# Four edits to a two-block transformer kernel: where the modulation product is made, in which order the score passes of differential attention run, where embedding and mixing are done, and how retention steps through its heads

## The chip, the cores and the metric

The kernel runs on one core of one Trainium2 chip, as one program of some twenty phases. The metric is the device time of one execution in microseconds (us), given as the median of three runs.

## The reference, cut to what matters

The sequence has 1,024 tokens of 1,024 float32 values. The first block is a mixing layer (differential and neighbourhood attention), a routed mixture of experts, and a gated embedding; the second block is two layers of retention and stick-breaking attention whose norm is modulated by a product of a condition vector.

```python
def diff_attention(...):          # 4 heads, two score maps of width 64 each
    s1 = einsum(q[..., 0, :], k1) * scale ; s2 = einsum(q[..., 1, :], k2) * scale
    w = softmax(s1) - lam * softmax(s2) ; o = w @ v
    return rms_norm(o, g_sub) * (1.0 - lam_init)

def first_block(...):
    h = h + concatenate([oa, ob]) @ w_out
    h = h + hier_moe(rms_norm(h, g_ffn), w_rg, w_re, w1, w3, w2)   # 2 of 32 experts a token
    h = h + rms_norm(p @ w_ple, g_ple) * sigmoid(rms_norm(h, g_plg) @ w_plg)

def hybrid_layer(x, c_act, ...):  # twice; c_act = silu(c)
    shift, scale, gate = split(c_act @ w_ada + b_ada, 3)           # w_ada: 1024 x 3072
    h = rms_norm_2(x, norm_g) * (1.0 + scale) + shift
    proj = h @ w_in
    y = concatenate([retention(...) * silu(rg), stick_breaking(...) * silu(sg)]) @ w_out
    return x + gate * y
# retention: 4 heads of 128, per head  o -> (o - mean(o)) * rsqrt(var(o) + eps)
```

## The kernel before, in words

All work is float32. A product that needs the accuracy is made as three passes over operands split into a high and a low part (`_hi`, `_lo`). Tokens go in 8 tiles of 128 (`NT`). Each phase opens its own buffers, gives each of the five engines one stream of instructions, written out by hand with semaphores between them, and ends with all engines waiting for each other. So nothing of a phase starts before the last instruction and the last waited-for transfer of the phase ahead. Names in the trace carry the tag of their phase: `da_` differential attention, `na_` neighbourhood attention, `rt_` router, `ex_` experts, `bt_` between, `ple_gate_`, `in_`, `ret_`, `stick_`, `out_`, `fin_`.

**Differential attention.** `score(i, t)` (L1204) makes the two score maps of one tile, c = 0 and c = 1, each of two 512-column halves `n` and three passes, into two pairs of PSUM banks. Map c waits for `exped[c]`, the exponential that reads the bank of the tile before. VectorE takes two maxima (L1310), ScalarE two exponentials (L1247), VectorE combines (L1324), TensorE turns the weights (L1229) and multiplies by v (L1237). `score(i+1, t+1)` stands in front of the turn and product of tile t. GpSimd lays the bias of the next phase (L1402) meanwhile.

**Router.** Per tile, TensorE turns the normed x (L687) and multiplies with 36 logit columns (L707). Behind the logits stand the modulation products (`modulate`, L695: 16 pieces of `w_ada`, 1,536 KB each, with 8 buffers, loaded by SyncE at L572), with the rank products (L718) after nine of them. VectorE ranks the experts; GpSimd then scatters 16 lots of slot rows (L628). **Experts** stream 192 MB of weights. **Between**, one tile after another, mixes the two expert rows of each token into h (L1801, L1806), makes `p @ w_ple` (L1764), its norm and gain (`factor`, L1822), and stores both; they are read again by the next phase.

**Gate phase** (`dense_phase` with tag `ple_gate`). For column block 0, tile t is loaded by GpSimd, squared on ScalarE (L221), its root taken (L224), scaled on VectorE in place (L315), turned on TensorE (L450), cast to the high part (L228), and subtracted for the low part (L326); then 24 matmuls a column block (L461 to L463). VectorE's order in the loop is take(t+1), scale(t+2), then the output of t. Column block 1 uses the kept operands.

**Retention.** Per head, in a loop: ScalarE copies the turned q and k, TensorE makes decayed scores, chunk products and outputs (L1898, L1905, L1914, L1917), and VectorE does the decay of q (L1961), the masked scores (L1966), the states (L1973, L1977), and the norm of the output in whole-head steps of 128x1024 (L1989 to L1997) and the gate (L2000). One set of buffers serves all heads.

## Time and profile before

| | |
|---|---|
| median of three runs | 3539.03 us (3537.36 to 3544.37) |
| profiled execution | 3547.53 us, span 3545.9 us |
| busy: TensorE / VectorE / ScalarE / GpSimd | 84% / 44% / 34% / 8% |
| differential attention | 310 to 593 us |
| router | 966 to 1078 us |
| experts | 1078 to 1684 us |
| between | 1684 to 1756 us |
| gate | 1756 to about 1889 us |
| retention, first and second layer | 2267 to 2350 and 3086 to 3169 us |

TensorE is busiest over the whole, but each phase has its own bound, and the phases do not overlap. So a change is to be read phase by phase, from the first instruction of one to the first of the next. Times of rows are from the start of the span. The profiled execution is 8.5 us longer than the median of the runs.

### The profile page before, as it was taken

Reading aid. Unit: us, or ns where it says so; the run is one execution under the profiler, and the core shown is the slowest. Engines: PE = TensorE matmul, PEld = TensorE weight load, DVE = VectorE, ACT = ScalarE, POOL = GpSimd, SP = SyncE. Lnnn points to the kernel's source line nnn. Section 1 sums busy time; section 2 is a strip of 40 time slices with the busy share of each in tenths; the row PEclk is TensorE's granted clock in tenths of the full one; section 3 lists DMA queues with packets and bytes.
Section 4 is the critical chain, followed back from the end, with each engine's and each line's share of the span. In section 5 each row is a group of like instructions: output and inputs, shape, how many; then the busy total and the mean of one; then the engine's idle time right before and its main releaser. Section 6 shows DMA issues by size and latency. Waiting matters only on the chain. (4 is left out here: it accounts for less than half of the span.)

```text
span 3545.9 us, 61528 instructions
## 1 busy us (share of the span) xinstructions
PE 2976.0 (84%) x22494; PEld 2317.5 (65%) x22494; DVE 1569.1 (44%) x2788; ACT 1199.3 (34%) x2129; POOL 276.9 (8%) x453
## 2 busy tenths in 40 slices
PE   7997876877876999998497999868877999868876
PEld 6786664655755888886275888644466888754455
DVE  4852656776131222221445411268844421068853
ACT  4332544665120110000253222148832222128841
POOL 0002600000022111111100000000000000000000
PEclk9998987988968999999798999879988999979998
DMA  5113112111397999998944222341044222241034
GB/s 178 68 71 105 27 25 94 35 56 54 118 372 281 394 395 394 395 394 309 348 156 163 93 96 72 117 133 33 10 158 158 103 95 74 99 145 35 25 116 163
DMA packets 244095, 545.93 MB, mean 154 GB/s; under 512 B 29196, under 2 KB 110896, under 8 KB 217240
## 3 DMA queue, kind: packets, MB, share of 16 engines
q1 hardware_dynamic: 213960, 460.23, 35.9%
q0 software_dynamic: 26720, 75.77, 6.5%
q10 hardware_dynamic: 3312, 8.59, 0.6%
q8 instruction: 60, 0.98, 0.1%
q14 instruction: 43, 0.35, 0.0%
HBM read 437.66 MB, written 107.79 MB: 154 GB/s over the span
## 5 line engine op out<-in xcount | busy, mean ns | idle before, releaser
L461 PE MATMUL ps<-in_wh,in_xh 128*128 (+1 forms) x1024 | 400.8, 391 | 0.0
L462 PE MATMUL ps<-in_wl,in_xh 128*128 (+1 forms) x1024 | 399.1, 390 | 0.0
L463 PE MATMUL ps<-in_wh,in_xl 128*128 (+1 forms) x1024 | 399.0, 390 | 0.0
L463 PEld LDWEIGHTS ps<-in_wh,in_xl 128*128 128x128 f32 x1024 | 192.7, 188 | 40.2
L462 PEld LDWEIGHTS ps<-in_wl,in_xh 128*128 128x128 f32 x1024 | 192.9, 188 | 39.8
L461 PEld LDWEIGHTS ps<-in_wh,in_xh 128*128 128x128 f32 x1024 | 192.8, 188 | 39.6
L1026 DVE TENSOR_TENSOR ex_hid<-ps,ex_act 32x128 f32<-32x128 f32 x96 | 28.2, 294 | 328.7 <-PE ps L1073 327.9
L461 PE MATMUL ps<-mix_in_wh,mix_in_xh 128*128 (+1 forms) x384 | 152.2, 396 | 9.1 <-DVE mix_in_out L381 5.6
L463 PE MATMUL ps<-mix_in_wh,mix_in_xl 128*128 (+1 forms) x384 | 150.1, 391 | 0.0
L462 PE MATMUL ps<-mix_in_wl,mix_in_xh 128*128 (+1 forms) x384 | 150.1, 391 | 0.0
L245 ACT COPY in_out<-ps 128x512 f32<-128x512 f32 x64 | 37.6, 588 | 248.3 <-PE ps L463 248.3
L304 DVE TENSOR_TENSOR in_wl<-in_raw,in_wh (+1 forms) x64 | 44.2, 690 | 159.9 <-ACT in_wh L216 159.7
L2325 DVE TENSOR_TENSOR stick_w<-stick_z,ps 128x256 f32<-128x256 f32 (+2 forms) x96 | 91.7, 955 | 52.2 <-PE ps L2159 50.6
L304 DVE TENSOR_TENSOR in_wl<-early,in_wh x64 | 43.1, 689 | 160.7 <-ACT in_wh L216 160.7
L1035 DVE COPY ex_y<-ps 32x256 f32<-32x256 f32 x96 | 41.0, 427 | 162.1 <-PE ps L1100 161.2
L206 POOL DMA_DIRECT2D out_x<-y x4 | 2.1, 528 | 1314.5 <-POOLq L36 1314.5
L461 PE MATMUL ps<-out_wh,out_xh 128*128 128x512 f32 x256 | 101.8, 398 | 0.9 <-DVE out_xl L326 0.9
L463 PE MATMUL ps<-out_wh,out_xl 128*128 128x512 f32 x256 | 100.5, 392 | 0.0
L462 PE MATMUL ps<-out_wl,out_xh 128*128 128x512 f32 x256 | 100.3, 392 | 0.0
L2318 DVE TENSOR_TENSOR stick_lo<-stick_soft,stick_hi 128x256 fp32r<-128x256 f32 (+2 forms) x96 | 91.6, 955 | 15.1 <-ACT stick_hi L2248 13.8
L988 ACT COPY ex_xT<-ps 128x768 f32<-128x768 f32 x33 | 26.4, 799 | 212.1 <-PE ps L1052 212.1
L2253 ACT ACTIVATE stick_w<-stick_w 128x256 f32<-128x256 f32 (+2 forms) x96 | 81.3, 847 | 46.0 <-DVE stick_w L2325 42.2
(409 smaller groups left out, 7433.7 us busy)
## 6 DMA issues: line engine op xcount, KB each, us to landing
ex_w_w1a<-in_w_dram SPq DMA_DIRECT2D x32, 1024.0 KB, 13.3
ex_w_w1b<-in_w_dram SPq DMA_DIRECT2D x32, 1024.0 KB, 14.4
ex_w_w3a<-in_w_dram SPq DMA_DIRECT2D x32, 1024.0 KB
ex_w_w3b<-in_w_dram SPq DMA_DIRECT2D x32, 1024.0 KB
ex_w_w2a<-in_w_dram SPq DMA_DIRECT2D x32, 1024.0 KB, 14.4
ex_w_w2b<-in_w_dram SPq DMA_DIRECT2D x32, 1024.0 KB
proj<-in_out SPq DMA_DIRECT2D x128, 256.0 KB, 2.0
rt_w_ada<-in_w_ada_dram SPq DMA_DIRECT2D x16, 1536.0 KB, 22.0
```

The lines of the kernel that those rows point to most:

```text
L206: pool.dma_start(x[p][:, 0:NK * P], src[p * P:(p + 1) * P, 0:NK * P]).then_inc(x_loaded[p], 16)
L245: act.copy(out[p][:], k.ps[:, 2 + p, :]).then_inc(out_ready, 1)
L304: dve.tensor_tensor(wl[:, c % 2, bass.ds(kt, 1), :], raw[c % 2][:, bass.ds(kt, 1), :], wh[:, c % 2, bass.ds(kt, 1), :].bitcast(F), ALU.sub ...
L461: pe.matmul(o, xh[:, kt, tok], wb[0], start=(kt == 0), stop=False)
L462: pe.matmul(o, xh[:, kt, tok], wb[1], start=False, stop=False)
L463: last = pe.matmul(o, xl[:, kt, tok], wb[0], start=False, stop=(kt == KT - 1))
L988: act.copy(xT[:].rearrange("p b k n -> p b (k n)"), psX).then_inc(x_taken, 1)
L1026: dve.tensor_tensor(hid[group(g), HM:], psH[1][BR:P, g * HQ:(g + 1) * HQ], act1[BR:P, g * HQ:(g + 1) * HQ], ALU.mult)
L1035: dve.tensor_copy(y[group(g), YM:], psY[BR:P, g * YQ:(g + 1) * YQ])
L2253: act.activation(ap, ap, ACT.Exp).then_inc(w_done, 1)
L2318: dve.tensor_tensor(lo[n % 2][:, :, cols(n)], soft[n % 2][:, :, cols(n)], hi[n % 2][:, :, cols(n)].bitcast(F), ALU.subtract).then_inc(lo_d ...
L2325: dve.tensor_tensor(w[n % 2][:, :, cols(n)], z[n % 3][:, :, cols(n)], psT[:, :, cols(n)], ALU.subtract).then_inc(weighed, 1)
```

## The change

Four edits, all of them moves or regroupings; what is computed stays.

1. The modulation product moves from the router to differential attention. It is cut into 32 pieces of 768 KB, one for each tile of each head, with 4 buffers. `modulate(h, t)` is 4 matmuls of 384 columns. Bias and gain are put on by GpSimd, which also stores the result.
2. The twelve score matmuls of a tile alternate between the two maps, whose operands lie on the lower and the upper 64 partitions, and all wait for both exponentials.
3. The phase between is gone. The embedding (`p @ w_ple`, norm, gain) goes into the router, its products behind the logits and behind the ranks. The mixing goes into the gate phase, on VectorE ahead of the square; the mixed x is stored by GpSimd, and the expert rows have one buffer each.
4. Retention keeps two sets of buffers and runs heads in pairs; the row statistics are taken by `bn_stats` and `bn_aggr`, and the normalised output is made by ScalarE.

```diff
@@ differential attention, TensorE
             def score(i, t):
-                for c in range(2):
-                    half = slice(c * DQK, (c + 1) * DQK)
-                    if not isinstance(i, int) or i > 0:
-                        pe.wait_ge(exped[c], i)
-                    for n in range(2):
-                        for i_pass, (q, kk) in enumerate(((q_hi, k_hi), (q_lo, k_hi), (q_hi, k_lo))):
+                if not isinstance(i, int) or i > 0:
+                    pe.wait_ge(exped[0], i)
+                    pe.wait_ge(exped[1], i)
+                for n in range(2):
+                    for i_pass, (q, kk) in enumerate(((q_hi, k_hi), (q_lo, k_hi), (q_hi, k_lo))):
+                        for c in range(2):
+                            half = slice(c * DQK, (c + 1) * DQK)
...
+            def modulate(h, kt):
+
+                pe.wait_ge(ada_loaded[kt % WB], 16 * (KT // WB * h + kt // WB + 1))
+                if kt == 0:
+                    pe.wait_ge(row_taken, h)
+                for g in range(GROUPS):
+                    last = pe.matmul(psM[g * GP:(g + 1) * GP, :], c_act[:, kt, :], wb[kt % WB][:, g * QN:(g + 1) * QN],
+                                     start=(kt == 0), stop=(kt == KT - 1))
+                last.then_inc(ada_used, 1)
...
                 for t in range(NT):
                     i = NT * h + t
+                    modulate(h, t)
                     if t + 1 < NT:
                         score(i + 1, t + 1)
@@ router, TensorE
+                if t % 2 == 1:
+                    pe.wait_ge(pr_loaded, 16)
+                    turn_p(t // 2)
...
-            for i in range(KT):
-                modulate(i)
-            pe.wait_ge(row_taken, 2)
-            modulate(KT)
+            pe.wait_ge(p_taken, NT // 2)
+            pe.wait_ge(w_p_loaded, 32)
+            embed(0)
+            embed(1)
...
-            for i in range(KT + 1, LAYERS * KT):
-                modulate(i)
+            for t in range(2, NT):
+                embed(t)
@@ router, VectorE
+            weigh(0)
             dve.wait_ge(ranked, 1)
...
+            for t in range(1, NT):
+                weigh(t)
@@ gate phase, GpSimd
+            if mixed:
+                for t in range(NT):
+                    p, own = t % 2, slice(t * P, (t + 1) * P)
+                    if t >= 2:
+
+                        pool.wait_ge(x_ready, t - 1)
+                        pool.wait_ge(x_saved[p], 16 * (t // 2))
+                    pool.dma_start(x[p][:], src[own, :]).then_inc(x_loaded[p], 16)
+                    if t >= 1:
+                        pool.wait_ge(x_mixed, t)
+                    for i in range(TOP_K):
+                        pool.dma_start(ye[i][:], k.slot_y[i * SEQ + t * P:i * SEQ + (t + 1) * P, :]).then_inc(ye_loaded, 16)
+                    if t >= 1:
+                        pool.dma_start(resid[(t - 1) * P:t * P, :], x[1 - p][:]).then_inc(x_saved[1 - p], 16)
@@ gate phase, ScalarE
             def scale(t, p, j):
                 if norm:
-                    act.wait_ge(x_loaded[p], 16 * (j + 1))
+                    if mixed:
+                        act.wait_ge(x_mixed, t + 1)
+                    else:
+                        act.wait_ge(x_loaded[p], 16 * (j + 1))
@@ gate phase, VectorE
                             take(2 * j + p + 1, 1 - p)
+                            mix(2 * j + p + 2, p, j + 1)
                             scale(2 * j + p + 2, p)
@@ retention, TensorE
+            turn(0)
+            score(0)
+            turn(1)
+            score(1)
+            for h in range(HR):
+                output(h)
+                if h + 2 < HR:
+                    turn(h + 2)
+                if h == 1:
+                    score(2)
+                    score(3)
@@ retention, VectorE
-                link(dve.tensor_reduce(sums[:], o, X, ALU.add))
-                link(dve.tensor_scalar(mu[:], sums[:], 1.0 / DR, None, ALU.mult))
-                link(dve.tensor_tensor(cen[:], o, each(mu[:]), ALU.subtract))
-                link(dve.tensor_tensor(sq[:], cen[:], cen[:], ALU.mult))
-                link(dve.tensor_reduce(var_sum[:], sq[:], X, ALU.add))
...
+                for t in range(a, b):
+                    last = dve.bn_stats(stats[p][:, t, :], psX[p][:, tile(t)])
+                last.then_inc(stats_done, 1)
+                dve.wait_ge(stats_done, u + 1)
+                for t in range(a, b):
+                    last = dve.bn_aggr(moments[p][:, t, :], stats[p][:, t, :])
...
@@ retention, ScalarE
+                for t in range(a, b):
+                    last = act.activation(nrm[p][:, tile(t)], psX[p][:, tile(t)], ACT.Identity, scale=rs[p][:, t:t + 1],
+                                          bias=shift[p][:, t:t + 1])
```

On TensorE in differential attention, at the first two tiles of a head, the program of before has all six score matmuls of one map and then all six of the other (`da_k_hi`, `da_q_lo` and so on are the high and low parts of k and q):

```order
L1204 MATMUL ps<-da_k_hi,da_q_hi 128x512
L1204 MATMUL ps<-da_k_hi,da_q_lo 128x512
L1204 MATMUL ps<-da_k_lo,da_q_hi 128x512
L1204 MATMUL ps<-da_k_hi,da_q_hi 128x512
L1204 MATMUL ps<-da_k_hi,da_q_lo 128x512
L1204 MATMUL ps<-da_k_lo,da_q_hi 128x512
```

The changed program has there:

```order
L1314 MATMUL ps<-da_k_hi,da_q_lo 128x512 x2
L1314 MATMUL ps<-da_k_lo,da_q_hi 128x512 x2
L1298 ISA
L1302 MATMUL ps<-da_w_ada,da_c_act 32x384 x4
L1308 REGISTER_ALU
L1314 MATMUL ps<-da_k_hi,da_q_hi 128x512 x2
L1314 MATMUL ps<-da_k_hi,da_q_lo 128x512 x2
```

Each pass now comes as a pair, one matmul for each map, and the four modulation matmuls stand between the scores of one tile and the next.

On VectorE in the gate phase, from the take of tile t+1 to the output of tile t, the program of before has:

```order
L326 ISA
L326 TENSOR_TENSOR ple_gate_xl<-ps,ple_gate_xh 128x8x128
L310 REGISTER_ALU
L311 ISA
L311 TENSOR_SCALAR ple_gate_ms<-ple_gate_ss 128x1
L313 ISA
L313 RECIPROCAL ple_gate_rs<-ple_gate_sd 128x1
L315 SCALAR_TENSOR_TENSOR ple_gate_x<-ple_gate_x,ple_gate_rs,ple_gate_gain 128x1024
```

The changed program has, from the second mixing step to the next take and mixing (`ple_gate_ye` are the expert rows, `ple_gate_xs` the scaled copy):

```order
L346 SCALAR_TENSOR_TENSOR ple_gate_x<-ple_gate_ye,slot_w,ple_gate_x 128x1024
L353 ISA
L353 TENSOR_SCALAR ple_gate_ms<-ple_gate_ss 128x1
L355 ISA
L355 RECIPROCAL ple_gate_rs<-ple_gate_sd 128x1
L360 SCALAR_TENSOR_TENSOR ple_gate_xs<-ple_gate_x,ple_gate_rs,ple_gate_gain 128x1024
...
L371 ISA
L371 TENSOR_TENSOR ple_gate_xl<-ps,ple_gate_xh 128x8x128
L342 ISA
L343 ISA
L343 SCALAR_TENSOR_TENSOR ple_gate_x<-ple_gate_ye,slot_w,ple_gate_x 128x1024
```

Two steps of 128x1024 stand now between the take and the mean square, which waits for ScalarE's square of what they make.

On VectorE in retention, at the end of a head, the program of before has:

```order
L1990 TENSOR_SCALAR ret_mu<-ret_sums 128x8
L1991 TENSOR_TENSOR ret_cen<-ps,ret_mu 128x1024
L1992 TENSOR_TENSOR ret_sq<-ret_cen 128x1024
L1993 TENSOR_REDUCE ret_var_sum<-ret_sq 128x8
L1994 TENSOR_SCALAR ret_ms<-ret_var_sum 128x8
L1996 RECIPROCAL ret_rs<-ret_sd 128x8
L1997 TENSOR_TENSOR ret_nrm<-ret_cen,ret_rs 128x1024
```

The changed program has, around the end of the first pair:

```order
L2005 SCALAR_TENSOR_TENSOR ret_shift<-ret_moments,ret_rs 128x8
L2013 TENSOR_TENSOR ret_y<-ret_nrm,ret_g 128x8x128
L1970 TENSOR_TENSOR ret_qTd<-ret_qT,ret_q_dec 128x1024
L1974 TENSOR_TENSOR ret_sm<-ps,ret_dec 128x512 x2
L1979 COPY ret_state<-ps 128x128
L1983 SCALAR_TENSOR_TENSOR ret_state<-ret_state,ret_t_dec,ps 128x128 x6
L2013 TENSOR_TENSOR ret_y<-ret_nrm,ret_g 128x8x128
```

The large centring, squaring and normalising steps are gone from VectorE, and the gate of one head stands beside the start of a later one.

## Rows read from the trace of the kernel before

**Rows 1.** By stretch: us, busy of PE, PEld, DVE, ACT, POOL, clock, DMA share, GB/s.

```profile
966.00:1078.00 112.00, 69.77 (x454) 49.43 (x454) 34.45 (x84) 23.60 (x40) 32.78 (x39) 0.63 0.82 318
1756.00:1889.00 133.00, 101.13 (x448) 82.70 (x448) 55.54 (x83) 60.12 (x85) 5.25 (x10) 0.87 0.50 168
2267.00:2350.00 83.00, 47.24 (x304) 44.09 (x304) 50.42 (x76) 15.13 (x26) 0.00 (x0) 0.75 0.43 133
```

**Rows 2.** Timeline of the phase between and its end: start, us, instruction [idle before].

```profile
1683.77 1.28 ACT L1777 ACT_TABLE_LOAD   x1 [17.00 <-PEq L36]
1695.87 1.28 DVE L1801 SCALAR_TENSOR_TENSOR bt_mid<-bt_expert,slot_w,bt_h 128x1024 f32<-128x1024 f32 x1 [18.98 <-DMA bt_expert<-slot_y]
1697.18 1.28 DVE L1806 SCALAR_TENSOR_TENSOR bt_out<-bt_expert,slot_w,bt_mid 128x1024 f32<-128x1024 f32 x1
1751.70 0.34 ACTq L1790 DMA_DIRECT2D ple<-bt_factor  x1
1756.33 1.28 ACT L262 ACT_TABLE_LOAD   x1 [6.18 <-PEq L36]
```

**Rows 3.** Tile view of the expert rows of the phase between.

```profile
DMA to landing us min/median/max: 4.9/9.1/11.9
```

**Rows 4.** Timeline of the gate phase: its start, then one tile's period.

```profile
1764.76 1.06 ACT L221 ACTIVATE ple_gate_junk<-ple_gate_x 128x1024 bf16<-128x1024 f32 x1 [4.96 <-DMA ple_gate_x<-h]
1773.83 0.77 PE L461 MATMUL ps<-ple_gate_wh,ple_gate_xh 128*128 128x512 f32 x1
1801.52 1.09 PE L450 MATMUL ps<-ident,ple_gate_x 128*128 128x128 f32 x8 [1.71 <-DVE ple_gate_x L315]
1803.66 1.06 ACT L221 ACTIVATE ple_gate_junk<-ple_gate_x 128x1024 bf16<-128x1024 f32 x1
1803.92 1.22 DVE L326 TENSOR_TENSOR ple_gate_xl<-ps,ple_gate_xh 128x1024 f32 x1
1805.31 1.28 ACT L224 ACT_TABLE_LOAD   x1 [0.51 <-DVE ple_gate_ms L311]
1808.48 1.09 PE L450 MATMUL ps<-ident,ple_gate_x 128*128 128x128 f32 x8 [0.41 <-DVE ple_gate_x L315]
```

**Rows 5.** Timeline of the router: last logits, modulation, ranks, last scatter, next phase.

```profile
1020.72 6.88 PE L707 MATMUL ps<-rt_wr,rt_xt 128*128 128x36 f32 x32
1042.72 0.70 PE L718 MATMUL ps<-rt_both,rt_tri 128*128 128x256 f32 x2
1056.08 2.79 PE L695 MATMUL ps<-rt_w_ada,rt_c_act 128*32 128x512 f32 x16 [0.89 <-DMA rt_w_ada<-in_w_ada_dram]
1071.49 0.96 POOL L628 DMA_INDIRECT slot_rows<-rt_tok,rt_slot  x1 [0.30 <-issue]
1078.44 1.28 ACT L1006 ACT_TABLE_LOAD   x1 [35.56 <-PEq L36]
```

**Rows 6.** Timeline of TensorE in the phase between: products of one tile.

```profile
1702.65 3.60 PE L1764 MATMUL ps<-bt_w,bt_xT 128*128 128x512 f32 x8
```

**Rows 7.** Timeline of differential attention: scores, maxima, next scores.

```profile
347.85 0.49 PE L1204 MATMUL ps<-da_k_hi,da_q_hi 64*128 64x512 f32 x1
348.01 0.39 PE L1204 MATMUL ps<-da_k_lo,da_q_hi 64*128 64x512 f32 x1
349.10 0.39 PE L1204 MATMUL ps<-da_k_lo,da_q_hi 64*128 64x512 f32 x1
350.51 2.35 DVE L1310 TENSOR_REDUCE da_neg_max<-ps 128x1 f32<-128x1024 f32 x2 [0.16 <-issue]
353.11 0.49 PE L1204 MATMUL ps<-da_k_hi,da_q_hi 64*128 64x512 f32 x1
```

**Rows 8.** Timeline of VectorE in retention, first layer: its steps, the last y.

```profile
2291.44 1.23 DVE L1992 TENSOR_TENSOR ret_sq<-ret_cen 128x1024 f32<-128x1024 f32 x1
2299.47 0.28 DVE L1973 COPY ret_state<-ps 128x128 f32<-128x128 f32 x1
2343.90 1.23 DVE L2000 TENSOR_TENSOR ret_y<-ret_nrm,ret_g 128x1024 f32 x1
```

More of the change, by code:

```diff
@@ L75, in dense_phase @@
 def dense_phase(nc, k, tag, src, w, dst, kinds, gain=None, shift=None, rope=None, head=None,
-                head_gain=None, resid=None, gate=None, times=None, order=None, after=None, turned=None):
+                head_gain=None, resid=None, gate=None, times=None, order=None, after=None, turned=None, mixed=False):
     C = len(kinds)
@@ L314, in scale @@
                     dve.wait_ge(x_rs, t + 1)
-                    last = dve.scalar_tensor_tensor(out=x[p][:], in0=x[p][:], scalar=rs[:, one], in1=gain_b[:],
+                    if mixed and (not isinstance(t, int) or t > 0):
+                        dve.wait_ge(x_turned, t)
+                    last = dve.scalar_tensor_tensor(out=xs[p][:], in0=x[p][:], scalar=rs[:, one], in1=gain_b[:],
                                                     op0=ALU.mult, op1=ALU.mult)
@@ L1176, in _ @@
                 load(i, [c * HA * DV for c in range(3)])
-            with sp.Fori(1, HA) as h:
-                first = [sp.snap(i * HA * DV + h * DV) for i in range(3)]
+            for i in range(WB):
+                load_ada(i)
+            for h in range(1, HA):
+                first = [i * HA * DV + h * DV for i in range(3)]
                 sp.wait_ge(turned, 4 * h)
@@ L1878, in _ @@
[L1878 to L1881 removed]
+            for h in range(HR - 2):
+                sp.wait_ge(kd_done, h + 1)
+                load(h + 2)
+            for u, (h, a, b) in enumerate(PARTS):
+                sp.wait_ge(y_done, u + 1)
+                sp.dma_start(part(dst[:, h * DR:(h + 1) * DR])[:, a:b, :], y[:, a:b, h * DR:(h + 1) * DR]).then_inc(stored, 16)
@@ L1883, in _, with turn @@
+            sp.wait_ge(stored, 16 * len(PARTS))
         @block.tensor
         def _(pe):
-            with pe.Fori(0, HR) as h:
+            def turn(h):
                 for i in range(2):
-                    pe.wait_ge(loaded[i], 16 * (h + 1))
+                    pe.wait_ge(loaded[h % 2][i], 16 * (h // 2 + 1))
                     for b in range(2):
-                        pe.wait_ge(taken, 4 * h + 2 * i)
+                        if 4 * h + 2 * i + b >= 2:
+                            pe.wait_ge(taken, 4 * h + 2 * i + b - 1)
@@ L1896, in _ @@
                 for t in range(NT):
-                    tok = slice(t * P, (t + 1) * P)
-                    last = pe.matmul(psS[:, tok], kT[:, tok], qT[:, tok], start=True, stop=True)
+                    last = pe.matmul(psX[p][:, tile(t)], kT[p][:, tile(t)], qT[p][:, tile(t)], start=True, stop=True)
                     if t % 4 == 3:
                         last.then_inc(scored, 1)
-                pe.wait_ge(loaded[2], 16)
+                if h == 0:
+                    pe.wait_ge(v_loaded, 16)
@@ L1915, in _ @@
                     if t:
                         pe.wait_ge(state_done, (NT - 1) * h + t)
-                        last = pe.matmul(psO[:, tok], qTd[:, tok], state[:, t, :], start=False, stop=True)
-                last.then_inc(product, 1)
+                        last = pe.matmul(psX[p][:, tile(t)], qTd[p][:, tile(t)], state[p][:, tile(t)], start=False, stop=True)
+                    if (h, t + 1) in [(of, b) for of, _, b in PARTS]:
+                        last.then_inc(product, 1)
+            turn(0)
```

538 lines of the change are left out of this document (253 added, 285 removed).

## The prediction

> **What bounds the kernel now.** I read the busy times by stretch first: as phases do not overlap, each change is priced as the length of its own phase. In the router TensorE is busy for 69.8 of 112 us, at a clock of 0.63, and the DMA engines for 0.82 of it; in the gate phase TensorE for 101 of 133 us; in retention the busiest engine, VectorE, for 50.4 of 83 us [rows 1]. So in retention no engine is the bound: a head is a chain, and what is to be seen is that one engine waits while another works. Next came the timelines. In between, the first mixing starts 12.1 us after the phase does (1683.77 to 1695.87) and waits for the expert rows; eight tiles later the phase ends at 1756.33 [rows 2]. In the gate phase one tile takes 6.96 us (1801.52 to 1808.48), and the rows of that period follow one another: turn, take, mean, table load and root, scale, turn [rows 4]. In the router the logits end at 1027.6, the ranks wait behind nine modulation products until 1042.72, and the scatters set the end: the last ends at 1072.45, the next phase starts at 1078.44 [rows 5]. In differential attention TensorE's last score ends at 349.49 and is wanted at 350.51 [rows 7]: 1.0 us to spare at full clock.
>
> **Between goes: -72.6 us.** The whole stretch from 1683.77 to 1756.33 [rows 2] is removed, with both end waits.
>
> **Gate phase: +27 us, of which +10.6 at the start.** Before, x lands at 1764.76, 8.4 us after the phase starts, and the first product is at 1773.83, 17.5 us after it [rows 4]. After, x and two expert rows must land (I take 10.3 us, between the 8.4 of x and the 12.1 of the first mixing in between), then two mixing steps run, 2.59 us (1695.87 to 1698.46) [rows 2]. The second tile's expert rows can only be fetched when the first has been mixed, since each has one buffer, so its mixing waits for a landing, then runs 2.59 us, and VectorE's take of the first tile stands behind it. 10.3 + 2.6 + 9.1 (median landing [rows 3]) + 2.6, then mean, root and scale (2 us), less what is not needed for the first product, put it at 28.1 us: +10.6. From then on, for each of five further tiles (the sixth hides partly in the start), the mixing adds 2.59 us to the chain, and ScalarE's square, which ran beside the take (1803.66, take 1803.92 [rows 4]), now waits for the mixing: about 1.35 with its read of 1.06 and the accumulator. That is 3.95 a tile, 19.7 for five, less 3 that the first turns gain from being later than their inputs: 16.7. Sum 27.3. The period becomes 11 to 12 us (6.96 plus 3.95, and more where a tile has a table load more). At 11.5 the expert rows have 11.5 - 2.6 = 8.9 us to come, about the median of 9.1 in a stretch whose DMA share was much higher than the gate's 0.50 [rows 1, 3], so I cost them at nothing; if they took 9.1 and their issue 1.1, each of six tiles would lose 1.3, and +8 is the bound above. A busier and longer stretch of waits lets the clock fall for some tiles: +2. Mixed x is stored by GpSimd's queue behind the expert rows' loads, where no one waits for it until the output of two tiles later. Range of the phase +22 to +45.
>
> **Router: +6.7 us.** Sixteen modulation products go, nine of which lay ahead of the ranks. In come four transposes for each two tiles in the logit loop, at the half clock that the stretch has (+3.9 us on the logits, which end near 1031.5), and two embeddings ahead of the ranks. An embedding of 8 matmuls takes 3.60 us in full clock [rows 6]; at half clock it is between that and 7.2; I take 5.8 for one and 3.6 for the other, as products of 512 columns raised the clock in the modulation's stretch, 9.4 for the two. So ranks stand at 1041 to 1042 rather than 1042.7 [rows 5], and the scatter chain ends where it did. But a second chain now ends later: six embeddings with two banks, each released by VectorE's `weigh`, which stands behind the slot chain and the block numbers, the long steps of 128x1728 among them, which I take as ending some 14 us after the ranks. `weigh(1)` is at about 1056, and six periods of 3.6 (one at 5.8, as the clock is low at first) end the last product at 1077.2; square, mean, root, inverse and gain add 3.3, and the last store to the next phase took 4.6 (1751.70 to 1756.33 [rows 2]). 1085.1 against 1078.4 is +6.7. With all at half clock it is +16 to +20; with the second chain hidden by the scatters, 0.
>
> **Experts: +1.** 2 MB of early weights are loaded at its end, with DMA full there.
>
> **Differential attention: +1.5 us, range 0 to +20.** Four 384-column matmuls a tile: 16 of 512 columns took 2.79 us at a high clock (1056.08) [rows 5], of which the columns here are 4 x 384 of 8,192 (the x16 row is 2 pieces of 8 with 512 and 256), so about 0.65 a tile. TensorE is free from 353.1 and must now wait for the second exponential too: the second maximum ends at 352.86 [rows 7] and a step of 128x1024 on ScalarE takes 1.06 [rows 4], so about 354.0. 0.65 fits in that gap. At half clock it is 1.3, and TensorE is on the path there. The alternation costs the early start of map 0 (0.9 us) and wins the overlap: the second map's first matmul starts at 347.85, before the last of the first, at 348.01 [rows 7], so two matmuls on different halves of the rows run together; six pairs at the 0.25 of one step (347.85 to 349.10 is five of them) end near 349.5, where the twelve singles did. So at full clock nothing is won and nothing lost; at half clock some tiles gain what the modulation costs. The Trainium skill ("TensorE: Matmul & The Clock Gate", What happens when you issue a matmul) says that matmuls stay in program order and only weight loads are pulled ahead. By that rule all of before would be twelve serial slots and after six. The trace disagrees for the start order in [rows 7]. By the rule the sum would be -20 us for this phase.
>
> **Retention: -13 us a layer, -26 for two.** Per head VectorE's five whole-head steps of 1.23 us (sums, centre, square, variance, normalise: 6.1 us) [rows 8] become 8 `bn_stats` of 128x128 out of PSUM. The trace has none; the nearest row is a copy of that shape, 0.28 us [rows 8], so 2.3 a head; 8 `bn_aggr` on six numbers, which I take as shorter than the copy, 0.17, 1.4; three small ones, 0.5. That is 4.2, and the normalise is on ScalarE, where there is room: 15 of 83 us busy [rows 1]; 8 activations of 128x128 with two operands of pointers, taken at 0.39, above the copy's 0.28, 3.1 a head, run beside the next head's steps. VectorE's work falls from 12.6 (a quarter of 50.4) to about 10.5 a head, 41 in all; and as heads go in pairs, what it waits, 32.6 us of the 83, shrinks to the start of the phase, 11, and its end, 5, and little more: 11 + 42 + 5 = 58 would be the least, and first and last heads, whose chains nothing covers, and ScalarE's normalising at the end make it 70. Followed step by step the last y ends at 2332 instead of 2345.1 [rows 8]: 13 us. The bounds: at 0.15 a `bn_stats`, -16; at 0.4 and 0.3 for the two kinds, 2 us a head more, -6. The Trainium skill ("VectorE: DVE Perf Modes", The TRN2 errata) says that each instruction pays a fixed latency; that speaks against 16 small steps in place of five long ones. By its figures for a PSUM source, an estimate is 0.26 us for one of 128 columns, against 0.28 in the row.
>
> **The sum.** -72.6 + 27.3 + 2 + 6.7 + 1 + 1.5 - 26 = -60.1 us. Against the profiled execution, 3547.5 us, that is 3487.4; the median lies 8.5 lower, so 3479, a change of -1.7%. What a measurement can tell from no change is about 0.2%, 7 us.
>
> **The rivals.**
> - The mixing costs what between cost. Place: gate phase, column block 0. If each tile waits for its expert rows (single buffer, 10.2 us from mixing end to mixing start, period 12.8), the cast and the root's table loads stand in series with it (+2.6 a tile) and the clock halves, the phase is +45 to +50, and the time about 3500. For it: 9.1 median [rows 3]. Against: DMA share 0.50 [rows 1]. Chance 0.18.
> - The router's second chain runs at half clock throughout, as the logits did (0.63 over the phase [rows 1]): +16 rather than +6.7, 3489; with it goes a dear `bn_stats` (3503 together). Chance 0.12.
> - The alternation pays, as the rule above has it: at half clock a slot is 0.5 us, twice the 0.25 above, six slots fewer are 3.0 us, and seven tiles that TensorE bounds give -20: 3459. Against: 347.85 before 348.01 [rows 7]. Chance 0.08.
> - Retention gains nothing, as `bn_stats` runs far slower than a copy (over 0.8 us for one): 3505. Chance 0.05.
> - Slower than before: in differential attention TensorE waits, with the scores queued behind it, for a modulation weight at every tile, or modulate pushes every score late. It decides from 60 / 32 = 1.9 us a tile beyond the 1.0 to spare. A tile takes some 6.4 us, and 768 KB in it are 120 GB/s, against the 318 that the router moved [rows 1], with four buffers. Chance 0.03.
> - As forecast: 0.54.
>
> **Range and chances.** The likeliest case's own range is 3466 to 3490. To leave out no more than 2 in 10 it must take in the first two rivals: 3455 to 3505. Faster 0.95, same 0.02, slower 0.03.
>
> **What would show it.** In the changed profile: no stretch between; the gate's turns of block 0 some 11.5 us apart, with the square behind the second mixing, and the idle before the mixing put down to the expert rows (the first rival) or not; the router's last factor store after the last scatter; ScalarE and VectorE overlapping in retention, `bn_stats` near 0.28 us, the phase near 70 us; differential attention still near 283 us, with pairs of scores about 0.25 us apart. The forecast is wrong if the gate phase is over 170 us, or if retention stays above 78.

## The result, and the profile after

| | before | changed |
|---|---|---|
| median | 3541.7 us (3537.4 to 3547.3, 4 runs) | 3489.5 us (3485.7 to 3491.5, 4 runs) |
| ratio | | 0.9843 (95% interval 0.9828 to 0.9858) |
| span of the profiled execution | 3545.9 us | 3489.2 us |

The kernel became faster by 52 us. The forecast was 60 us, at 3479, in a range of 3455 to 3505. The two profiled executions lie 56.6 us apart (3547.53 and 3490.98), and it is with them that the phases below add up. Lengths of phases, from the first instruction of one to that of the next, in the two traces:

| phase | before | after | difference | forecast |
|---|---|---|---|---|
| differential attention | 282.5 | 285.4 | +2.9 | +1.5 |
| router | 112.5 | 116.8 | +4.3 | +6.7 |
| experts | 605.3 | 610.0 | +4.7 | +1 |
| between | 72.6 | none | -72.6 | -72.6 |
| gate | 128.8 | 169.1 | +40.3 | +29.3 |
| retention, both layers | 165.4 | 133.1 | -32.3 | -26 |
| all others | | | -4.1 | 0 |
| sum | | | -56.8 | -60.1 |

The gate phase became 40.3 us longer, and with 169.1 us it is only 1 us under the 170 that the forecast named as its sign of being wrong.

The stretches of the changed kernel that answer to those of [rows 1], in the same columns (router, gate, first and second retention, differential attention):

```profile
966.00:1083.00 117.00, 76.10 (x278) 55.42 (x278) 42.94 (x104) 34.87 (x65) 25.12 (x34) 0.68 0.37 138
1693.00:1862.00 169.00, 111.13 (x448) 90.65 (x448) 74.48 (x96) 57.22 (x80) 16.95 (x32) 0.79 0.61 202
2245.00:2312.00 67.00, 39.93 (x304) 37.76 (x304) 35.68 (x124) 26.32 (x58) 0.00 (x0) 0.81 0.56 165
3046.00:3111.00 65.00, 40.32 (x304) 38.04 (x304) 35.68 (x124) 26.27 (x58) 0.00 (x0) 0.79 0.57 170
311.00:597.00 286.00, 206.60 (x1472) 151.78 (x1472) 172.09 (x313) 131.74 (x251) 116.78 (x175) 0.87 0.46 140
```

In the gate phase the mean clock fell from 0.87 to 0.79, and in retention VectorE is busy for 35.7 us instead of 50.4 [rows 1]. The timeline of the gate phase, one period of column block 0 in the changed kernel, merged from three engines, against that of [rows 4]:

```profile
1762.09 1.97 PE L498 MATMUL ps<-ident,ple_gate_xs 128*128 128x128 f32 x8 [5.09 <-DVE ple_gate_xs L360]
1764.19 1.01 ACT L258 CAST ple_gate_xh<-ps 128x1024 f32 x1 [1.35 <-PE ps L498]
1765.37 1.23 DVE L371 TENSOR_TENSOR ple_gate_xl<-ps,ple_gate_xh 128x1024 f32 x1 [0.92 <-ACT ple_gate_xh L258]
1766.51 1.28 DVE L343 SCALAR_TENSOR_TENSOR ple_gate_x<-ple_gate_ye,slot_w,ple_gate_x 128x1024 f32<-128x1024 f32 x1
1767.95 1.28 DVE L346 SCALAR_TENSOR_TENSOR ple_gate_x<-ple_gate_ye,slot_w,ple_gate_x 128x1024 f32<-128x1024 f32 x1 [0.16 <-DVE ple_gate_x L343]
1769.36 1.06 ACT L251 ACTIVATE ple_gate_junk<-ple_gate_x 128x1024 bf16<-128x1024 f32 x1 [4.15 <-DVE ple_gate_x L346]
1770.90 1.28 ACT L254 ACT_TABLE_LOAD   x1 [0.39 <-DVE ple_gate_ms L353]
1772.72 1.28 DVE L360 SCALAR_TENSOR_TENSOR ple_gate_xs<-ple_gate_x,ple_gate_rs,ple_gate_gain 128x1024 f32<-128x1024 f32 x1
1774.06 1.97 PE L498 MATMUL ps<-ident,ple_gate_xs 128*128 128x128 f32 x8 [3.63 <-DVE ple_gate_xs L360]
```

It is one chain, with no more than 0.2 us between most of its steps: turn, cast, take, two mixings, square, table load and root, scale, turn, in 11.97 us. Nobody waits for a transfer. The mixing and the square stand in it as forecast; the turn takes 1.97 us, not the 1.09 of [rows 4]. The start of the phase, and the one later tile that waited for its expert rows (VectorE, changed kernel):

```profile
1705.91 1.28 DVE L343 SCALAR_TENSOR_TENSOR ple_gate_x<-ple_gate_ye,slot_w,ple_gate_x 128x1024 f32<-128x1024 f32 x1 [7.97 <-DMA ple_gate_ye<-slot_y]
1715.24 1.28 DVE L343 SCALAR_TENSOR_TENSOR ple_gate_x<-ple_gate_ye,slot_w,ple_gate_x 128x1024 f32<-128x1024 f32 x1 [1.19 <-DMA ple_gate_ye<-slot_y]
1741.27 1.28 DVE L343 SCALAR_TENSOR_TENSOR ple_gate_x<-ple_gate_ye,slot_w,ple_gate_x 128x1024 f32<-128x1024 f32 x1 [2.49 <-DMA ple_gate_ye<-slot_y]
```

The first mixing is 12.6 us after the phase's start at 1693.35 (10.3 taken). The turns of TensorE show how the whole column block differs. The second and the third turn of the kernel before, then those of the changed kernel:

```profile
1772.21 1.97 PE L450 MATMUL ps<-ident,ple_gate_x 128*128 128x128 f32 x8 [2.25 <-DVE ple_gate_x L315]
1784.30 1.97 PE L450 MATMUL ps<-ident,ple_gate_x 128*128 128x128 f32 x8 [3.65 <-DVE ple_gate_x L315]
```

```profile
1721.02 1.97 PE L498 MATMUL ps<-ident,ple_gate_xs 128*128 128x128 f32 x8 [7.36 <-DVE ple_gate_xs L360]
1734.27 1.97 PE L498 MATMUL ps<-ident,ple_gate_xs 128*128 128x128 f32 x8 [4.83 <-DVE ple_gate_xs L360]
```

From the second turn to the eighth there are six periods. Before, they are 12.1, 9.0, 8.2, 7.0, 8.3 and 7.0 us long (51.5 in all); in the changed kernel 13.3, 14.6, 13.3, 12.0, 13.3 and 12.0 (78.3). The first grew by 1.2 us, the second by 5.5, the last four by 5.0 each. In the last four, the turns took 1.0 to 1.1 us before and 1.97 after.

The router's end, in the order of its two chains: last scatter, then the third embedding, the five last embeddings in one run, last factor, next phase:

```profile
1070.11 0.95 POOL L638 DMA_INDIRECT slot_rows<-rt_tok,rt_slot  x1 [0.30 <-issue]
1044.60 5.40 PE L720 MATMUL ps<-rt_w_p,rt_pT 128*128 128x512 f32 x8 [1.78 <-DVE rt_factor L784]
1055.74 19.19 PE L720 MATMUL ps<-rt_w_p,rt_pT 128*128 128x512 f32 x40 [5.74 <-DVE rt_factor L784]
1077.05 1.28 DVE L784 SCALAR_TENSOR_TENSOR rt_factor<-ps,rt_p_rs,rt_gain_p 128x1024 f32<-128x1024 f32 x1
1083.36 1.28 ACT L1041 ACT_TABLE_LOAD   x1 [6.54 <-PEq L36]
```

The scatters end at 1071.1, 7 us ahead of the last factor: the second chain ends the phase. In differential attention (TensorE, one tile) the passes come as pairs, 0.24 us apart once running, with the modulation of 0.85 us ahead of them in what was idle time:

```profile
360.76 0.85 PE L1302 MATMUL ps<-da_w_ada,da_c_act 128*32 128x384 f32 x8
362.03 0.49 PE L1314 MATMUL ps<-da_k_hi,da_q_hi 64*128 64x512 f32 x2 [0.41 <-ACT da_e L1360]
362.33 0.42 PE L1314 MATMUL ps<-da_k_hi,da_q_lo 64*128 64x512 f32 x2
362.57 0.42 PE L1314 MATMUL ps<-da_k_lo,da_q_hi 64*128 64x512 f32 x2
```

In retention the new steps, by source line (duration least, median, most), and one head's normalising on ScalarE:

```profile
L1991 DVE BATCH_NORM_STATS2 ret_stats<-ps x64: 278/281/302, 2271.8 to 3104.1; 128x6 f32<-128x128 f32 x64
L1995 DVE BATCH_NORM_AGGREGATE ret_moments<-ret_stats x64: 145/149/183, 2273.5 to 3104.6; 128x2 f32<-128x6 f32 x64
```

```profile
2271.77 1.68 DVE L1991 BATCH_NORM_STATS2 ret_stats<-ps 128x6 f32<-128x128 f32 x8 [1.02 <-PE ps L1904]
2273.48 0.64 DVE L1995 BATCH_NORM_AGGREGATE ret_moments<-ret_stats 128x2 f32<-128x6 f32 x8
2283.16 2.90 ACT L1943 ACTIVATE ret_nrm<-ps,ret_shift,ret_rs 128x128 f32<-128x128 f32 x8 [0.47 <-DVE ret_shift L2005]
2307.24 0.69 DVE L2013 TENSOR_TENSOR ret_y<-ret_nrm,ret_g 128x512 f32<-128x512 f32 x1 [0.97 <-ACT ret_nrm L1943]
```

One `bn_stats` takes 0.281 us, but eight take 1.68, since each starts before the one ahead has ended.

### The profile page after: what moved, and what is told of

Its sections match the earlier page's. It is cut to its first block and busy times, and to the rows that moved or that the text cites. A ratio compares the mean times of both kernels' runs of the same rounds, so it can differ in the third digit from the quotient of the medians.

```text
span 3489.2 us, 61320 instructions
## 1 busy us (share of the span) xinstructions
PE 2927.1 (84%) x22494; PEld 2278.4 (65%) x22494; DVE 1540.2 (44%) x2880; ACT 1222.0 (35%) x2193; POOL 298.2 (9%) x489
## 5 line engine op out<-in xcount | busy, mean ns | idle before, releaser
L2344 DVE TENSOR_TENSOR stick_lo<-stick_soft,stick_hi 128x256 fp32r<-128x256 f32 (+2 forms) x96 | 91.7, 955 | 14.9 <-ACT stick_hi L2274 13.6
```

Source lines behind the costliest of these rows:

```text
L2344: dve.tensor_tensor(lo[n % 2][:, :, cols(n)], soft[n % 2][:, :, cols(n)], hi[n % 2][:, :, cols(n)].bitcast(F), ALU.subtract).then_inc(lo_d ...
```

## The experiments

**Retention alone.** The kernel before, with the retention phase of the changed kernel put in its place.

```diff
@@ kernel before
-def retention_phase(...):   # one set of buffers, heads in a loop
+def retention_phase(...):   # that of the changed kernel, word for word
```

> The kernel before with the retention phase of the changed kernel alone. My theory: both retention phases shorten by what they shorten in the changed kernel, 82.3 to 67.2 and 83.1 to 65.9 us, and nothing else moves: -32 us, 0.991 of before. Rival (phases lend each other clock or DMA queues, so that the gain is partly given back in the stick-breaking phases behind): under -25 us.

Ratio 0.9894 (0.9878 to 0.9911), 3513.8 against 3550.1 us: -36. The two phases are 67.7 and 66.9 us long (82.3 and 83.1 before). The sum of both is -30.8, and nothing behind them is longer, so the rival is refuted. The two profiled executions are 32.5 us apart (3547.5 and 3515.0), so 5 of the 36 us are not in the traces: the 3550.1 is from other executions of the kernel before. Where those 5 us lie is not shown. The edit gives what it gives in the changed kernel (-32.3), and does so without the others.

**Alternating scores alone.** The kernel before, with `score` of the changed kernel.

> The kernel before with the alternating score passes alone. My theory: TensorE already runs the two maps side by side where it can, and at full clock VectorE and ScalarE set the 6.36 us of a tile: the phase stays at 282 us, within 3 us. Rival (program order is strict, before had twelve serial slots): the half-clock tiles gain 2.6 to 3 us each, the phase falls to about 262 us, the time by 20 us.

```diff
@@ kernel before, score(i, t)
-                for c in range(2):
-                    ...
-                        pe.wait_ge(exped[c], i)
+                    pe.wait_ge(exped[0], i)
+                    pe.wait_ge(exped[1], i)
...
+                        for c in range(2):
```

Ratio 0.9994 (0.9984 to 1.0003). The phase is 283.9 us long, 282.5 before. The alternation does save time on TensorE: at full clock the twelve scores of a tile take 2.7 us before (346.75 to 349.49) and 1.65 us here in pairs. First and last pair:

```profile
356.10 0.50 PE L1205 MATMUL ps<-da_k_hi,da_q_hi 64*128 64x512 f32 x2 [1.20 <-ACT da_e L1249]
357.33 0.42 PE L1205 MATMUL ps<-da_k_lo,da_q_hi 64*128 64x512 f32 x2
```

TensorE's busy time in the phase falls from 215.0 to 182.4 us. But it only waits for what it has saved (first waits of TensorE in this phase, in all, times, longest; this kernel, then the kernel before):

```profile
PE ps L1205 <- ACT da_e L1249: 41.6, 28, 3.7
```

```profile
PE ps L1204 <- ACT da_e L1247: 6.1, 4, 1.5
```

TensorE waits 35 us more for the exponentials, and the tile takes as long: 6.36 us from one maximum to the next in both kernels, and the first two tiles of a head, where the clock is low, 13.6 to 14.0 us before and 13.4 to 14.1 here. So the 20 us of the rival did not come. That alone would not refute the rule of strict order, since TensorE does not set the pace here. The rows of the kernel before do. At a tile ahead of the rise of the clock it has:

```profile
333.65 0.62 PE L1204 MATMUL ps<-da_k_lo,da_q_hi 64*128 64x512 f32 x1
333.76 0.94 PE L1204 MATMUL ps<-da_k_hi,da_q_hi 64*128 64x512 f32 x2
334.36 0.77 PE L1204 MATMUL ps<-da_k_hi,da_q_lo 64*128 64x512 f32 x2
334.78 0.77 PE L1204 MATMUL ps<-da_k_lo,da_q_hi 64*128 64x512 f32 x2
```

Each x2 is one matmul of either map (the weights of the one at 333.76 waited for the second map's semaphore). The first of map 1 starts at 333.76 and runs beside the last three of map 0, which stand ahead of it in the program; the twelve take nine steps here (332.63 to 336.06). So matmuls on different halves of the rows did overtake each other, and before, the two maps already ran side by side where their turns met.

**Scores map after map in the changed kernel.** The reverse of it.

```diff
@@ changed kernel, score(i, t)
-                        for c in range(2):
...
+                for c in range(2):
+                    half = slice(c * DQK, (c + 1) * DQK)
+                    if not isinstance(i, int) or i > 0:
+                        pe.wait_ge(exped[c], i)
```

> The changed kernel with the score passes of before, map after map, the first map waiting for its own exponential only. My theory: within 3 us of the changed kernel, differential attention at 283 to 289 us. Rival (alternation makes the room for the modulation products): it rises by 10 us or more, to over 295 us.

Ratio 0.9909 (0.9892 to 0.9925), 3516.9 us: some 23 us dearer than the changed kernel (0.9843 of its own kernel before). Differential attention is 286.6 us long, within what I expected. The 23 us are in the phase behind it: neighbourhood attention has 285.4 us instead of 262.6, though no line of it differs. Its TensorE waits, and the packets of the instruction queue over the whole execution, in this kernel:

```profile
PE ps L1636 <- issue: 23.8, 3, 8.3
```

```profile
q8 instruction: 89, 1.46, 0.2%
```

and in the changed kernel:

```profile
q8 instruction: 62, 1.02, 0.1%
```

TensorE waits at the first instruction of its loop over heads, three times, 7.5 to 8.3 us each, for nothing that the profile shows. 27 packets more, 0.44 MB, were fetched by the queue: nine in each of the three later passes of the loop, where the changed kernel has none. The loop is the same; the program ahead of it is 8 TensorE instructions shorter, since a score of the changed kernel needs one more for its second wait (in differential attention the traces hold 3,105 TensorE instructions against 3,137, which is 8 in each of four passes). That gave a theory on the place of the code, to be tested.

**The same, moved back by 8 instructions.**

```diff
@@ the kernel of the last run
-            pe.wait_ge(c_done, 1)
+            for _ in range(16):
+                pe.wait_ge(c_done, 1)
             with pe.Fori(0, HA) as h:
```

> The changed kernel with the score passes map after map, as in the run that took 22 us more, plus 16 waits on a semaphore that is long done, ahead of the head loop of differential attention, so that TensorE's later instructions stand 8 places further back, exactly where the changed kernel has them. My theory: the 22 us were TensorE's loop over heads in neighbourhood attention fetching its instructions anew in three of four passes (7.5 to 8 us each, 89 instruction packets instead of 62), which the place of the loop in memory decides and not the order of the scores: neighbourhood attention back at 262 to 265 us, 62 packets, the time within 5 us of the changed kernel. Rival (the order of the scores did it): neighbourhood attention stays at 285 us.

The trace holds 8 TensorE instructions more ahead of the head loop. Neighbourhood attention takes 260.7 us, and the queue has 62 packets; the ratio is 0.9846 (0.9824 to 0.9868), and the changed kernel beside it on the same chip 0.9843. So the 23 us were the place of a loop in the program. The order of the scores is worth nothing in the time that can be measured in either kernel.

**Pairs with the old statistics.** The changed kernel, with the sum, centre, square, sum and normalise steps of before on VectorE.

```diff
@@ changed kernel, retention, VectorE
-                for t in range(a, b):
-                    last = dve.bn_stats(stats[p][:, t, :], psX[p][:, tile(t)])
+                link(dve.tensor_reduce(sums[:, a:b], o, X, ALU.add))
+                link(dve.tensor_tensor(cen[:, a:b, :], o, each(mu[:, a:b]), ALU.subtract))
+                link(dve.tensor_tensor(sq[:, a:b, :], cen[:, a:b, :], cen[:, a:b, :], ALU.mult))
...
```

> The changed kernel with heads in pairs, but the statistics of before on VectorE (sum, centre, square, sum, normalise over a whole head) and no normalising on ScalarE. It splits the 32 us of retention between the pairing and the statistics. My theory: VectorE is the bound once heads are paired, so the five steps of 1.23 us against bn_stats and bn_aggr (1.7 + 0.6) cost it about 3.8 us a head more: each phase 67 + 14 = about 80 us, so nearly all of the gain comes from the statistics. Rival: the pairing alone hides the waits, which were 32 us of 83, and each phase stays under 73 us.

The phases are 77.3 and 77.0 us long. From 82.3, pairing takes 5 us (6 in the second layer); from 77.3 to 67.2 the statistics and the move of the normalising take 10 (11). Its stretch shows why it stops there:

```profile
2243.60:2321.00 77.40, 42.07 (x304) 39.90 (x304) 51.38 (x85) 15.27 (x27) 0.00 (x0) 0.76 0.48 143
```

VectorE has the same 51 us of work as before, in a phase whose first 9 and last 5 us it cannot use, and between them it waits 9.6 us more, 5.0 of them for the scores. My theory put too much on the statistics (80 us foreseen), the rival too much on the pairing (under 73). The one execution of this kernel took 3511.1 us, 21.6 above the changed kernel, where the two phases differ by 21.2.

**TensorE kept at work in the gate phase.**

```diff
@@ changed kernel, gate phase, TensorE, ahead of turn(t + 1)
+                    for _ in range(12):
+                        pe.matmul(k.ps[:, 6, :], xh[:, 0, 0:P], wh[...], start=True, stop=True)
```

> The changed kernel with twelve more matmuls of 512 columns into an unused bank ahead of each turn of the gate phase's first column block (from tile 2 on); their result is not read. My theory: the turns ran at half clock (1.97 us each instead of 1.09) because TensorE waits 3.6 to 5.9 us ahead of each. With these it idles less, the clock is granted, and the period falls by about 1 us, from 13.0 to 12.0: the phase 169 to about 163 us. Rival (the clock is not set by what stands ahead of the turn, or the added work delays it): 169 us or more.

This kernel, the next three, the one with the second norm sooner and the one with the old statistics were executed once each. Their whole times (here 3492.4 us, then 3486.9, 3478.2 and 3479.2) cannot tell a few us, since the phases that no edit touches differ by some us from trace to trace; what is read is the length of the phase. Six traces of kernels with this gate phase untouched have it 167.0 to 169.3 us long, 168.4 in the mean.

The phase is 166.4 us long, 169.1 in the changed kernel and 168.3 when that ran again: 2 to 3 us less, not 6. From the second turn to the eighth it is 77.2 us, against 78.3 and, when the changed kernel ran again, 77.5. Most turns still took 1.97 us. One of those that did not, and the one behind it:

```profile
1773.66 1.09 PE L498 MATMUL ps<-ident,ple_gate_xs 128*128 128x128 f32 x8 [1.11 <-DVE ple_gate_xs L360]
1786.06 1.97 PE L498 MATMUL ps<-ident,ple_gate_xs 128*128 128x128 f32 x8 [3.11 <-DVE ple_gate_xs L360]
```

The same two turns in the second trace of the changed kernel, which has no added matmuls:

```profile
1775.97 1.09 PE L498 MATMUL ps<-ident,ple_gate_xs 128*128 128x128 f32 x8 [3.96 <-DVE ple_gate_xs L360]
1788.37 1.97 PE L498 MATMUL ps<-ident,ple_gate_xs 128*128 128x128 f32 x8 [4.26 <-DVE ple_gate_xs L360]
```

Both periods are 12.40 us; the same one in the first trace of the changed kernel, from a turn of 1.97 (1774.06) to 1787.33, is 13.27. The 0.87 is the turn's. So the clock's price is 0.9 us a tile, shown. That the added matmuls raised the clock at any turn is not shown, since that turn ran at full clock without them too. What decides the clock there stays open.

**Two buffers for each expert row.**

```diff
@@ changed kernel, gate phase
-            ye = [s.sb(f"ye{i}", [P, DM]) for i in range(TOP_K)]
+            ye = [[s.sb(f"ye{i}", [P, DM])[:] for i in range(TOP_K)],
+                  [k.early[:, 2 * i:2 * i + 2, :].rearrange("p k n -> p (k n)") for i in range(TOP_K)]]
```

> The changed kernel with two buffers for each expert row of the gate phase (the second in the space of the early weights, whose load for the next phase moves behind column block 0). My theory: the chain of turn, cast, take, mixing, square, root and scale sets the period, and only the second tile and tile 3 waited for expert rows (1.2 and 2.5 us): the phase falls by 3 to 6 us, to 163 to 166. Rival of the prediction (single buffers make the mixing as dear as in the phase between): it falls by 15 us or more.

The phase is 164.4 us long: -4.7. The second turn is 8.04 us behind the first instead of 9.33, and the wait of tile 3 is gone. The periods in the middle stay (13.27 and 11.97). Of the 4.7 us, 0.9 are one turn at full clock, as in the second trace of the changed kernel (168.3). So single buffers cost about 4 us, and not the 15 of the rival. The phase behind, whose early weights are now loaded later, is no longer for it (382.5 us, 382.4 in the changed kernel).

**Mixing ahead of the take.**

```diff
@@ changed kernel, gate phase, VectorE
-                            take(2 * j + p + 1, 1 - p)
                             mix(2 * j + p + 2, p, j + 1)
+                            take(2 * j + p + 1, 1 - p)
                             scale(2 * j + p + 2, p)
```

> The changed kernel with the mixing of tile t+2 ahead of the take of tile t+1 on VectorE, one buffer for each expert row as it was. My theory: the mixing then runs while TensorE turns and ScalarE casts, and the square beside the take, so 3.9 us of the period leave the chain, but expert rows (5.8 us median after an issue of 1.1) now come late for a period of 9 us: period 10 to 11, phase 150 to 158 us. Rival (single buffers are the bound): phase not under 165 us.

158.3 us: -10.8 (-10.1 from the mean of 168.4), just above the upper end of what I expected. Expert rows are now waited for at seven tiles, 18.6 us in all (VectorE):

```profile
DVE ple_gate_x L343 <- DMA ple_gate_ye<-slot_y: 18.6, 7, 8.0
```

**Both together.**

> Both: mixing ahead of the take and two buffers for each expert row. My theory: period 9 to 9.5 us, phase about 143 to 148 us, 20 to 25 us under the changed kernel. Rival (x itself, which must be stored before its buffer is loaded again, is then late): phase 150 us or more, with VectorE waiting for x at the mixing.

150.4 us, -18.7 (-18.0 from the mean), 2 us longer than foreseen. From the third turn on the turns are 9.9 to 10.6 us apart instead of 12.0 to 14.6:

```profile
1733.41 1.10 PE L505 MATMUL ps<-ident,ple_gate_xs 128*128 128x128 f32 x8 [0.89 <-DVE ple_gate_xs L367]
1744.00 1.19 PE L505 MATMUL ps<-ident,ple_gate_xs 128*128 128x128 f32 x8 [4.01 <-DVE ple_gate_xs L367]
```

Neither edit alone gives this: -4.7 and -10.8 are 15.5, and together they give 18.7. The shorter period is what makes the second buffer needed: with one buffer VectorE waited 18.6 us for expert rows, with two 10.2, of which 8.1 are at the start (VectorE in this kernel; `early` is the second buffer):

```profile
DVE ple_gate_rs L362 <- ACT ple_gate_sd L261: 11.0, 8, 1.7
DVE ple_gate_x L350 <- DMA ple_gate_ye<-slot_y: 8.6, 2, 8.1
DVE ple_gate_x L350 <- DMA early<-slot_y: 1.6, 3, 0.7
```

The phase is as long as the rival had it, but not for its reason: VectorE waits at most 0.7 us for a transfer at any later tile. The period is now VectorE's own round: 7.3 us of work, 1.74 us of waiting for table load and root, and the rest in waits of 0.5 us or less, 10.3 in all, where I had 9 to 9.5. TensorE's turn is off it: in the version below the turns from the third on take 1.10 and 1.97 us by turns, and the phase is as long.

**The second embedding's norm sooner.**

```diff
@@ changed kernel, router, VectorE
+            weigh(1)
             link(dve.tensor_tensor(past[:], ...))          # block numbers
...
-            for t in range(1, NT):
+            for t in range(2, NT):
                 weigh(t)
```

> The changed kernel with the second embedding's norm and gain on VectorE ahead of the block numbers instead of behind them. My theory: the chain of factors, not the scatters, ends the router; it starts 4.6 us sooner and the scatters are then next, so the router falls by 4 to 6 us, from 116.8 to about 112. Rival (the clock or the products set the chain's pace, so that it ends where it did): under 1 us.

The router is 116.1 us long, against 116.8 and 117.7 in two traces of the changed kernel. Nine traces of kernels with this router untouched have 116.8 to 119.4 us, 118.2 in the mean, so the edit is worth 1 to 2 us and not the 4 to 6 of my theory. TensorE's rows of this kernel say why:

```profile
1057.74 3.70 PE L720 MATMUL ps<-rt_w_p,rt_pT 128*128 128x512 f32 x8 [1.16 <-DVE rt_factor L784]
1064.13 15.70 PE L720 MATMUL ps<-rt_w_p,rt_pT 128*128 128x512 f32 x32 [2.69 <-DVE rt_factor L784]
```

One product came forward into the bank that was free, and the next waited again for VectorE, which was now in the block numbers. The chain moved by one product and not as a whole: TensorE's idle time ahead of the last five products is 3.9 us instead of 5.7 (1055.74, above). A third bank, or the block numbers behind more than one of the norms, was not tried.

**The version that the runs point to**, and the changed kernel beside it on one chip.

> The version the runs point to: mixing ahead of the take, two buffers for each expert row, and the second embedding's norm ahead of the block numbers. My theory: 18.7 us of the gate phase and 4.5 of the router add up: 3466 to 3471 where the changed kernel has 3489.5, ratio to before about 0.978. Rival (the phases behind give part of it back): above 3476.

> The changed kernel itself on the chip of these runs, for the comparison with them: 0.984 of before.

3474.7 us, ratio 0.9796 (0.9775 to 0.9816); the changed kernel 3490.2, 0.9843 (0.9822 to 0.9864). That is 15.5 us faster than the change, and 71 us faster than before. The gate phase is 150.4 us long as in the run of its two edits (17.9 less than in the changed kernel's trace beside it), the router 115.9 (1.8 less). The time is 4 us above the range that I expected (3466 to 3471) and below the rival's 3476; the interval, 3466 to 3481 us, does not decide between them.

## Why the prediction was right, and where it was off

The direction, the size and the largest terms held, but that the sum came within 4 us of the traces' 56.8 is in part luck: the gate phase, the experts and differential attention came out 16 us dearer than foreseen, and the router, retention and the phases that I had put at nothing 13 us cheaper. In its own steps:

- **Between goes, -72.6.** The phase is gone; of its transfers the early weights stand in the expert phase (below).
- **Gate phase, +29.3 foreseen, +40.3 measured.** The mechanism was the forecast one: the mixing and the square stand in the chain, and a period without a second table load takes 11.97 us. What was mis-sized is the per-tile sum. I had 3.95 us for five tiles, less 3 for the first turns, and 2 for the clock: 18.7. The six periods grew by 26.8. Five of them paid in full, as counted: 5.0 us each in the last four, of which 0.9 are the turn at half clock and 4.1 the mixing and the square; 5.5 in the second, where the expert rows came 2.5 us late. The 3 us of the first turns did not come off; the first period grew by 1.2 instead. That is 4.2 us. The clock was 3.5 us and not 2, and the rest of the five tiles 2.4: together 8.1 of the 11 us. The start was 11.8 us dearer and not 10.6, with the first product 29.3 us after the phase's start. (The terms that I wrote down for it add up to 26.6, not to 28.1, and lack square and turn; the first expert rows came later than taken, 12.6 for 10.3, and the second sooner, 6.7 for 9.1.) The last 1.7 us lie behind the eighth turn, where I had nothing. The likeliest rival (mixing as dear as in between, +45 to +50) comes near the size. Its halved clock came true on the turns, its waits for expert rows at every tile did not.
- **Router, +6.7 foreseen, +4.3 measured.** The second chain ends the phase, as forecast: last factor 1078.3, next phase 5.0 later. The rank products start at 1041.6, as foreseen. What was mis-sized is the number of products behind `weigh(1)`: I counted six, but the third embedding ran at 1044.6 in the bank that `weigh(0)` had freed, and five followed, in one run at 3.8 us each. They end at 1074.9 instead of 1077.2, which is the difference. (My own terms, 1056, 5.8 and five times 3.6, make 1079.8 and not 1077.2.)
- **Differential attention, +1.5 foreseen, +2.9 measured,** within the spread of this phase between traces of kernels with the same code in it (281.8 to 288.4). The modulation fits in the idle time (0.85 us a tile, 0.65 foreseen). The alternation is worth nothing in time: shown alone (0.9994) and undone. The rival that it pays is refuted, since TensorE waits for the exponentials as long as it has saved.
- **Retention, -26 foreseen, -32.3 measured.** The Trainium skill ("VectorE: DVE Perf Modes", The TRN2 errata) has a fixed cost for each instruction, which spoke against small steps. The estimate of 0.26 us from its figures is near what a single `bn_stats` takes (0.281 us for 128 columns), but it does not hold for a run of them: eight come 0.20 us apart (1.68 us), and eight `bn_aggr` 0.07 us (0.64), so a head pays 2.32 us for sixteen steps, where I had 3.7. That is the step that was mis-sized: 1.4 us a head, at most 5.5 a layer, and more than covers the 3.1 a layer by which I was off. VectorE's work is 35.7 us a layer and not 41; why not all of the 5.5 shows in the phase is open. The old statistics in the paired kernel gave 10 to 11 of the 15 to 17 us back, so most of the gain is in this step and in the move of the normalising.
- **Experts, +1 foreseen, +4.7 measured.** The early load is issued at 1673.20, while the last weights still land, and the phase ends 20.5 us after its last weight issue instead of 18.1: 2.4 us. The eleven traces of kernels with this early load have 605.4 to 610.5 us, 608.4 in the mean, and the three without it 605.0 to 605.8. So the phase is about 3 us longer; that the early load is the cause is argued and not shown.
- **All others, 0 foreseen, -4.1 measured.** 2.6 us of it are in neighbourhood attention, which takes 265.2 to 265.4 us in three traces with the old differential attention ahead of it and 260.5 to 264.7 in those with the new one (but for the kernel of 285.4). Why is open.

## What to carry to other kernels

When work is moved into a chain, its price there is its duration in every period in which that chain is the bound (here five of six), plus what it un-hides (here the square), plus what TensorE's steps in it cost where the clock is lower (here 0.9 us a turn). A saving on an engine that only waits longer for it is worth nothing (the alternation: 33 us of TensorE's time). Where an engine waits at a fixed point of a loop, put the moved step in that wait (mixing ahead of the take: 10 to 11 us, and 18 to 19 with a second buffer). And before a difference is put down to an edit, look in which phase it lies: 23 us between two kernels with one edit in differential attention lay in another phase, whose code was the same.

## What the runs showed of the hardware that was not expected

- The place of a loop in TensorE's program costs time. Eight instructions fewer ahead of the loop over heads in neighbourhood attention made three of its four passes begin with a wait of 7.5 to 8.3 us, with nine packets on the instruction queue in each of them, where otherwise only the first pass has any; 8 instructions put back removed both. In the waits this shows as "issue" at the first instruction of a loop.
- Matmuls on different halves of the rows overtook each other: the first of map 1 started at 333.76, beside the last three of map 0, which stand ahead of it in the program. Twelve scores in pairs took 1.65 us, one map after the other 2.7 us.
- `bn_stats` of 128x128 out of PSUM takes 0.281 us for one, and the next starts after 0.20 us; `bn_aggr` 0.149 and 0.07.
- ScalarE's activation of 128x128 with scale and bias from memory takes 0.46 us for one and starts every 0.34 us in a run (eight in 2.90 us).
